# Two transformer blocks on one core: the front's order of work, the attention's turns, and constant products in TensorE's waits

## The reference

```python
# first block: layer 0 (MLA) and layer 1 (sliding window)
mem_n = rmsnorm(mem, mem_norm_g)
proj = rmsnorm(x, attn_norm_g[0]) @ mla_w_in           # 384 q rank, 256 kv rank, 32 rope, 256 cross
q  = rmsnorm(c_q, q_norm_g) @ w_uq                     # 12 heads of 64 + 32 rope
kv = rmsnorm(c_kv, kv_norm_g) @ w_ukv                  # 12 heads of 64 + 64
mix = softmax(causal(q k^T)) v                         # rope on q and on one shared key part
cross = softmax(q_cross (mem_n @ w_mem_kv)_k^T) (...)_v  # 4 heads over 256 memory rows
x = x + concat(mix, cross) @ w_o
x = x + relu(rmsnorm(x) @ w_up)**2 @ w_down            # 4096 hidden
# layer 1: the same with window attention, alibi, sinks
x = rmsnorm(x, final_norm_g)
# second block: m = silu(c) @ ada_w + ada_b gives shift, scale, gate
# layer 0: convolutions and RG-LRU, then w_out; swiglu ffn of 2816
# layer 1: qkv (1024 -> 3072), stick-breaking attention of 16 heads, w_out; swiglu ffn
```

## Time and profile before

| | us |
|---|---|
| median of 3 runs | 1308.36 |
| lowest and highest | 1306.59 and 1308.95 |
| the profiled execution | 1304.23 |
| its span | 1302.1 |
| TensorE busy | 1230.4 |
| VectorE busy | 875.4 |
| ScalarE busy | 639.2 |
| GpSimd busy | 116.9 |

### The profile page before, as it was taken

One profiled execution on the slowest core, in us unless ns is written; L12 is line 12 of the kernel. 1 busy time (PEld: TensorE's weight loads), 2 busy tenths in 40 slices (PEclk: granted clock), 3 DMA queues, 4 the chain that ended last, 5 costly groups with the idle time before them and its releaser, 6 DMA issues.

```text
span 1302.1 us, 21705 instructions
## 1 busy us (share of the span) xinstructions
PE 1230.4 (94%) x8765; PEld 1149.4 (88%) x8765; DVE 875.4 (67%) x1130; ACT 639.2 (49%) x839; POOL 116.9 (9%) x178
## 2 busy tenths in 40 slices
PE   6779999999999999999889989999979998999998
PEld 6768899988897999989789989998868778999987
DVE  5565588777885697778787677774576556554453
ACT  6526566633236566633447344433355674444332
POOL 0000001110115011111100001100000240000000
PEclk9889999999999999999989889999989999999999
DMA  8432368786862388777733548865645304456452
GB/s 308 147 108 75 127 215 290 285 291 247 277 228 91 103 284 289 256 287 267 267 121 139 165 146 272 289 218 164 220 141 193 131 1 129 136 188 193 133 177 76
DMA packets 150000, 249.83 MB, mean 192 GB/s; under 512 B 5505, under 2 KB 80618, under 8 KB 149930
## 3 DMA queue, kind: packets, MB, share of 16 engines
q1 hardware_dynamic: 135810, 198.21, 45.2%
q0 software_dynamic: 13952, 50.60, 10.7%
q10 hardware_dynamic: 168, 0.04, 0.0%
HBM read 247.79 MB, written 1.05 MB: 191 GB/s over the span
## 4 chain that ended last, share of the span: by engine, by line
PE 88%; DVE 6%; ACT 3%; issue 2%; ACTq 0%; POOL 0%; DVEq 0%; POOLq 0%
PE ps L1861 19%; PE ps L1862 19%; PE ps L1863 19%; PE ps L1881 14%; PE ps L1883 7%; DVE w_lo L1109 2%; PE ps L2128 2%; PE ps L1995 1%; PE ps L2110 1%; PE ps L2313 1%; PE ps L1926 1%; PE ps L2286 1%; PE ps L2097 1%; PE ps L1916 1%; PE ps L2323 1%
## 5 line engine op out<-in xcount | busy, mean ns | idle before, releaser
L1861 PE MATMUL ps<-h_hi,w_hi 128*128 128x256 f32 x1648 | 473.8, 287 | 19.9 <-issue 14.6
L1109 DVE TENSOR_TENSOR w_lo<-raw,w_hi 128x2048 fp32r<-128x2048 f32 (+4 forms) x196 | 412.3, 2144 | 116.3 <-ACT w_hi L703 116.1
L1862 PE MATMUL ps<-h_lo,w_hi 128*128 128x256 f32 x1648 | 470.4, 285 | 0.0
L1863 PE MATMUL ps<-h_hi,w_lo 128*128 128x256 f32 x1648 | 470.2, 285 | 0.0
L703 ACT ACTIVATE w_hi<-raw 128x2048 fp32r<-128x2048 f32 (+4 forms) x196 | 341.2, 1790 | 190.0 <-PE ps L1883 129.7
L1861 PEld LDWEIGHTS ps<-h_hi,w_hi 128*128 128x128 f32 x1648 | 318.8, 193 | 22.1 <-issue 18.7
L1862 PEld LDWEIGHTS ps<-h_lo,w_hi 128*128 128x128 f32 x1648 | 318.9, 193 | 0.1
L1863 PEld LDWEIGHTS ps<-h_hi,w_lo 128*128 128x128 f32 x1648 | 318.6, 193 | 0.1
L1881 PE MATMUL ps<-a_both,w_hi 128*128 128x512 f32 x800 | 283.7, 398 | 0.0
L1883 PE MATMUL ps<-a_both,w_lo 128*128 128x256 f32 x800 | 224.8, 281 | 0.0
L1881 PEld LDWEIGHTS ps<-a_both,w_hi 128*128 128x128 f32 x800 | 150.4, 188 | 36.5
(11 more groups left out here) (367 smaller groups left out, 1445.5 us busy)
## 6 DMA issues: line engine op xcount, KB each, us to landing
ada_raw<-in_l_ada_w POOLq DMA_DIRECT2D x96, 512.0 KB, 6.8
raw<-in_mlp_w_up SPq DMA_DIRECT2D x32, 1024.0 KB, 7.3
raw<-in_mlp_w_down SPq DMA_DIRECT2D x32, 1024.0 KB, 6.9
raw<-in_l_ffn_w_gate SPq DMA_DIRECT2D x22, 1024.0 KB, 5.5
raw<-in_l_ffn_w_up SPq DMA_DIRECT2D x22, 1024.0 KB, 8.0
raw<-in_l_ffn_w_down SPq DMA_DIRECT2D x16, 768.0 KB, 6.0
raw<-in_l_w_qkv SPq DMA_DIRECT2D x12, 1024.0 KB, 6.3
raw<-in_l_w_in SPq DMA_DIRECT2D x10, 1024.0 KB, 6.4
```

The costliest lines, as they stand in the source:

```text
L1109: nc.vector.tensor_tensor(w_lo[:, s.slot, cut], raw[:, s.slot, cut], w_hi[:, s.slot, cut].bitcast(F32), ALU.subtract).then_inc(split_lo, 1)
L1861: nc.tensor.matmul(to, sh, mh, start=first, stop=False, skip_group_check=True)
L1862: nc.tensor.matmul(to, sh, ml, start=False, stop=False, skip_group_check=True)
L1863: return nc.tensor.matmul(to, sl, mh, start=False, stop=last, skip_group_check=True)
```

## The change

SP loads `mem0` in two halves, each as soon as half of the first slot is split. `kvn` has squares of its own (`sq_kv`). On ScalarE and VectorE the front's norms are cut into steps (squares, sums, variance, root, scaling, high parts) and dealt out among the splits and copies. `w_uq` and `w_ukv` alternate between two pairs of banks. `mem0` and `mem1` go chunk by chunk. Silu is made from Exp on ScalarE and a reciprocal on VectorE; the sines move behind the last `kv_rows_out`. `mix_turn` waits for one group per pair. ScalarE makes the exponentials of heads 16 and 17 before it copies `swa_v`, and `down0`'s tenth slot (the second of `swa`) is split earlier, on VectorE in halves around `delayed_var`. `warm_up` and `keep_warm` put products of constants or of weights, whose results nobody reads, in TensorE's queue.

```diff
# SP
-            load(Slot("mem0", 0), k_major(a["w_mem_kv"][0]))
+            for half in range(2):
+                sp.wait_ge(split_lo, 2 * half + 2)
+                cut = slice(half * KD // 2, (half + 1) * KD // 2)
+                sp.dma_start(ring(raw, mem_slot.slot, KD, BANK)[:, cut, :], w_mem[:, cut, :]).then_inc(raw_loaded[mem_slot.slot], 16)
...
# ScalarE
             nc.scalar.activation(cqT[:, 0:2, :], acc(0).rearrange("p (c t) -> p c t", c=2), ACT.Copy).then_inc(acc_out[0], 1)
+            wait_source(act, "qn")
+            squares_of("qn")
             split(Slot("mem0", 0))
...
-            norm("qn", meanwhile=lambda: split(Slot("w_uq", 0)))
+            act.wait_ge(acc_out[0], turn("w_in", 1) + 1)
+            squares_of("kvn")
+            root_of("qn")
+            split(Slot("w_uq", 0), (0,))
+            high_of("qn")
+            split(Slot("w_uq", 0), (1,))
...
+            mem_keys("mem0", mem_k0)
+            root_of("kvn")
+            split(Slot("w_ukv", 0), (0,))
+            high_of("kvn")
+            q_rows_out(0)
+            split(Slot("w_ukv", 0), (1,))
+            q_rows_out(1)
+            small_columns()
+            q_rows_out(2)
+            split(Slot("mem1", 0), (0,))
+            kv_rows_out(0)
+            split(Slot("mem1", 0), (1,))
+            kv_rows_out(1)
+            kv_rows_out(2)
+            trigonometry()
...
             delayed_pair("attn1", 2)
+            split(Slot("down0", 9))
             delayed_pair("attn1", 3)
-            split(Slot("down0", 9))
...
             split(Slot("swa", 4))
+            exp_head(16)
+            exp_head(17)
             wait_part(Slot("swa", 3), 1)
...
-            heads(16, 32)
+            heads(16, 32, begun=2)
# VectorE
+            sums_of("qn")
             split(Slot("mem0", 0))
+            row_low(1, 0, m_hi, m_lo)
+            row_low(1, 1, m_hi, m_lo)
+            wait_part(Slot("w_in", 1), 1)
+            nc.vector.tensor_scalar(qx0[:, 1, :], ps[:, 1, 0:T], -HD ** -0.5, None, ALU.mult)
+            nc.vector.tensor_copy(kropeT[:, :], ps[0:ROPE, 1, T:2 * T]).then_inc(acc_out[1], 1)
+            row_low(1, 2, m_hi, m_lo)
+            row_low(1, 3, m_hi, m_lo)
+            variance_of("qn")
+            sums_of("kvn")
+            scaled("qn")
+            split(Slot("w_uq", 0))
+            mem_values("mem0", mem_v0)
+            variance_of("kvn")
+            scaled("kvn")
+            q_rows_out(0)
             split(Slot("w_ukv", 0))
             q_rows_out(1)
+            vector_constants()
+            trigonometry()
             q_rows_out(2)
+            split(Slot("mem1", 0), (0,))
+            kv_rows_out(0)
+            split(Slot("mem1", 0), (1,))
+            small_columns()
+            kv_rows_out(1)
+            kv_rows_out(2)
...
-                ada_group_done(ADA_GROUP[f"down{l}"] + 4)
+                if l:
+                    ada_group_done(ADA_GROUP["down1"] + 4)
...
+            split(Slot("down0", 9), (0,))
             delayed_var("attn1")
-            split(Slot("down0", 9))
+            split(Slot("down0", 9), (1,))
# TensorE
+UQ_BANKS, UKV_BANKS = ((4, 5), (0, 1), (4, 5)), ((0, 1), (4, 5), (0, 1))
+            def keep_warm(phase, n, bank=WARM_BANK):
+                s = Slot(phase, 0)
+                w = ring(w_hi, s.slot, s.kc, s.cols)
+                pe.wait_ge(split_lo, s.split + 2)
+                for _ in range(n):
+                    nc.tensor.matmul(ps[:, bank, 0:T], w[:, 0, 0:P], w[:, 1, 0:T], start=True, stop=True, skip_group_check=True)
+            def warm_up(n):
+                for _ in range(n):
+                    nc.tensor.matmul(ps[:, 1, 0:P], ones[:, :], ident[:, :], start=True, stop=True, skip_group_check=True)
...
+            warm_up(18)
             turn_rows(0, rows_x)
+            warm_up(6)
             as_chunks_arrive("w_in", "attn0")
...
-            memory("mem0", between="qn")
+            norm_sum_all("qn")
+            memory = [("features", (0, P)), ("rows", CROSS, CROSS, ((0, 0), (1, T)))]
+            as_chunks_arrive("mem0", "mem", work=memory, hi=m_hi, lo=m_lo, sums_after=1, sums="kvn")
...
                     for tile in range(NT):
-                        wait_acc(tile, turn(phase, g))
-                        token_rows(s, ps[:, tile, 0:n], tile, g * n, n, hi, lo).then_inc(parts_done, 1)
+                        if (phase, g) != ("w_uq", 0):
+                            wait_acc(tile, turn(phase, g) - 1)
+                        token_rows(s, ps[:, banks[g][tile], 0:n], tile, g * n, n, hi, lo).then_inc(parts_done, 1)
...
             for q in range(4):
+                if q == 2:
+                    for tile in range(NT):
+                        wait_acc(tile, turn("w_ukv", 1) + 1)
                 turn_pair(2 + q, lambda ch, t: x_again[:, t, (2 * q + ch) * P:(2 * q + ch + 1) * P]).then_inc(turned, 1)
-            memory("mem1")
+            as_chunks_arrive("mem1", "mem", work=memory, hi=m_hi, lo=m_lo)
...
+                if not begun:
+                    warm_up(4)             # in heads, after the first two scores
...
-                pe.wait_ge(o_copied, copied)
                 for q in range(4):
+                    pe.wait_ge(o_copied, copied - 3 + q)
                     turn_pair(2 + q, lambda ch, t: rows_from[:, t, (2 * q + ch) * P:(2 * q + ch + 1) * P]).then_inc(mix_turned, 1)
+            wait_acc(1, turn("mem1", 0) + 1)
+            warm_up(4)                     # ahead of the heads
...
+            keep_warm("lru_in", 6)
             norm_sum_all("final")
...
+            keep_warm("lru_in", 48)
             as_chunks_arrive("lru_in", "mix0")
...
+            keep_warm("lru_out", 20, NORM_BANK)
             as_chunks_arrive("lru_out", 2, order=LRU_PAIRS)
...
+                keep_warm(f"gate_up{l}", 11)
                 norm_sum_all(f"ffn{l}")
+                keep_warm(f"gate_up{l}", 36)
...
+            keep_warm("qkv", 5)
             norm_sum_all("mix1")
+            keep_warm("qkv", 36)
```

More of the change, by code:

```diff
@@ L142 @@
 FIRST_UP_BANKS = (2, 3)
+WARM_BANK = 3
+UQ_BANKS, UKV_BANKS = ((4, 5), (0, 1), (4, 5)), ((0, 1), (4, 5), (0, 1))
 LRU_ORDER = (4, 1, 2, 3, 0)
@@ L824, in _, with kv_rows_out @@
[L824 to L828, removed]
+            def kv_rows_out(g):
                 act.wait_ge(parts_done, Slot("w_ukv", 0).before + 2 * g + 1)
-                kv = acc(0).rearrange("p (h d) -> p h d", h=4)
+                kv = acc(UKV_BANKS[g][0]).rearrange("p (h d) -> p h d", h=4)
                 nc.scalar.activation(k_rows[:, 0, 4 * g:4 * g + 4, 0:HD], kv[:, :, 0:HD], ACT.Copy)
@@ L877, in sink_sums, with heads @@
                 nc.scalar.activation(sinkexp[:, :, :], sinkexp[:, :, :], ACT.Exp).then_inc(sink_exp, 1)
-            def heads(first, last):
+            def heads(first, last, begun=0):
                 for hc in range(first, last + 1):
-                    if hc < last:
+                    if first + begun <= hc < last:
                         exp_head(hc)
@@ L1146, in norm @@
                 wait_source(dve, name)
[L1147 to L1152 removed]
+                l, which = MODULATED[name]
+                gain_of = lambda ch: modg[:, l, which, ch:ch + 1]
                 def low(q):
@@ L1407, in _ @@
             nc.vector.tensor_copy(ckvT[:, 0, :], ps[:, 1, T:2 * T]).then_inc(acc_out[1], 1)
+            sums_of("qn")
             split(Slot("mem0", 0))
-            vector_constants()
-            for q in range(4):
-                row_low(1, q, m_hi, m_lo)
-            def during_qn():
-                wait_part(Slot("w_in", 1), 1)
-                nc.vector.tensor_scalar(qx0[:, 1, :], ps[:, 1, 0:T], -HD ** -0.5, None, ALU.mult)
-                nc.vector.tensor_copy(kropeT[:, :], ps[0:ROPE, 1, T:2 * T]).then_inc(acc_out[1], 1)
-                split(Slot("w_uq", 0))
-                trigonometry()
@@ L1421, in _ @@
-            norm("qn", between=during_qn)
-            def q_rows_out(g):
-                dve.wait_ge(parts_done, Slot("w_uq", 0).before + 2 * g + 2)
-                nc.vector.tensor_scalar(q_rows[:, 1, 4 * g:4 * g + 4, :], ps[:, 1, 0:4 * QK].rearrange("p (h d) -> p h d", h=4),
-                                        -QK ** -0.5, None, ALU.mult).then_inc(acc_out[1], 1)
-            def during_kvn():
-                mem_values("mem0", mem_v0)
-                q_rows_out(0)
-            norm("kvn", between=during_kvn)
+            row_low(1, 0, m_hi, m_lo)
@@ L1944, in four_blocks, with as_chunks_arrive @@
                     two_bank_slot(phase, j)
-            def as_chunks_arrive(phase, name, work=None, order=range(4), hi=h_hi, lo=h_lo, sums_after=None, banks=(0, 1)):
+            def keep_warm(phase, n, bank=WARM_BANK):
[7 more added lines that the diff above has]
+                    nc.tensor.matmul(ps[:, 1, 0:P], ones[:, :], ident[:, :], start=True, stop=True, skip_group_check=True)
```

(3 more changed lines are left out.)

160 lines of the change are left out of this document (89 added, 71 removed).

## The result

The changed kernel took 1271.56 us (median of 4 runs, 1270.63 to 1273.65) where the kernel before took 1308.65 (median of 4, 1306.59 to 1308.99): a ratio of 0.9722, 95% interval 0.9705 to 0.9739. Measured again on another chip it was 1272.44 against 1305.88: 0.9744 (0.9729 to 0.9759). The first measurement gives 37.1 us, the second 33.4. The prediction was 1278 (1269 to 1290), faster. Of the 32 timed executions of the kernel before, two took 1331.5 and 1333.3 us at a mean granted clock of 0.956 and 0.954, and no comparison here uses them.

The account below looks back on a forecast made before the run. TensorE, busy 94% of 1302.1 us, was taken as the bound, with only its waits and lower-clock time to win. Front 18.7, attention 5.5 and fillers 6.3 make 30.5; 1308.4 - 30.5 = 1278, range 1269 to 1290.

Parts of the forecast that it names:

- the offset of 4.1: Whole kernel: the runs' median is 4.1 us above the profiled execution, carried over to the forecast of 1278.
- rival B: Front: new waits overlap or vanish; front 23 to 25, fillers 8, 38 us in all, so 1270; chance 0.14.
- the 6.8: Front, at 53.4: TensorE's wait of 6.8 us behind ScalarE's `mem_k`, forecast to go entirely.
- The new waits: Front: waits the change itself brings to TensorE, behind splits, banks and copies; 6.7 us with the last copy.
- the last copy: Front's end, before the first scores: TensorE waits 0.7 us for it, counted among the new losses.
- 71.9: Front: TensorE's work between the first product (14.89) and 112.2, products and transposes together, 71.9 us of 97.3.
- the 25.4 reckoned: Front: time TensorE loses in the kernel before, in waits and at half rate, 25.4 us of a 97.3 stretch.
- Rival A: Front: in-order queues bite more than walked; front 12, total 20 to 24 us, so 1286; chance 0.16.
- Rival D: Front: norm, split and copy chain only displaced, `w_ukv` and `mem1` wait as long; 1289; chance 0.07.
- between the front and the end no DMA is on the chain: After the front: no transfer binds, so a shift won at the front is kept to the end.
- rival E: Norms, `lru_out`, start: fillers run at half rate and outlast their waits, costing 20 us; kernel slower; chance 0.04.
- Rival C: Norms: fillers don't hold the clock and win nothing; the rest, 24 to 25 us, stands; 1284; chance 0.07.

Follow-up runs that it names:

- the second trace: The unedited changed kernel profiled and timed once more, on another chip: 1272.44 us, against 1305.88 for the kernel before.
- `swa_kT` first: Against the changed kernel, VectorE scales `swa_kT` before the products with `ada_raw` and not behind them: 1271.58 us.

## Why the prediction came out as it did

**The sum.** It said 30.5 us; the profiled executions are 30.6 apart, the medians 33.4 and 37.1. Two things lie between 30.6 and 37.1. The profiled execution of before was 4.4 below its median (4.1 by the median that the prediction had), and that of the changed kernel 2.1 above its own. The failed step is the one that took the offset of 4.1 us over to the kernel after. What the runs show in its place is that the offset goes with the clock, and the change brings the clock to 0.995 to 0.998: the executions of before that took 1305.8 us and more ran at a mean granted clock of 0.975 to 0.978, those near the profile at 0.979 or 0.980. An estimate: 0.0035 of 1305 us is 9.1 us more at half rate, which costs up to 4.6. That this half rate lay behind the waits is argued and not shown, for no trace of an execution at 0.975 was kept. The 2.1 is the changed kernel's own spread; 1.1 of it is what `qkv`'s fillers lost in that execution and not in the repeated one. The median lies nearer to rival B's 1270, but not by B's way: the front gave 20.3 and not 23, the fillers 5.2 and not 8.

That 30.5 met 30.6 is in part luck. By the traces the span became 30.1 shorter: the front gave 20.3 for 18.7, the attention 5.4 for 5.5, the fillers 5.2 for 6.3, and 0.85 was lost in `w_o0`, which the sum didn't have.

**Front: 19.1 to the first scores, measured 20.4.** First product 13.88 (predicted 13.8), `w_uq` straight behind `mem0` at 51.59 (51.6), the 6.8 gone. The new waits were 6.7 and came to 2.9: `cqT` 0.4 (0.7), `v_rows` 0.9 (2.0), `mla_qT` 1.6 (1.7), none for `w_ukv`'s split (1.0), its banks (0.6) and the last copy (0.7). The clock did not fall before `mem1` (0.7). Those 4.5 did not all come out as gain, because the term for TensorE's work was too small. From the first product to the first scores the changed kernel takes 78.0 us; without the 2.9 of waits and 1.1 of fillers that is 74.0 of work, where the sum had 71.9. The part that the trace shows best: `w_uq`'s products are 0.173 us apart and not 0.16, `w_ukv`'s 0.23 and not 0.215, 1.2 together. So less was idle before than the 25.4 reckoned, and the wait for `w_ukv`'s split is hidden: the split ended when I said, 61.2, and TensorE got there at 61.39. The fillers ahead of the scores take the last 1.1. Rival A (queues bite more) had the right places and the wrong size; moving two entries of the queues took the remaining 2.5 out and showed that the order was the cause. Rival D is refuted by the 51.59.

**Attention: 5.5, measured 5.4.** The turns gave 1.1, 1.1 and 2.0 (predicted 1.0, 1.0, 1.3), the exponentials 1.0 (1.2). The split gave 1.4 (1.0), and 1.1 of it was lost at once at the first scores. Here a second step failed: that "between the front and the end no DMA is on the chain". VectorE stands before the transfer of `ada_raw` with the scaling of `swa_kT` behind it in its queue. It did so in the kernel before too, for 1.81 us, but there the first scores waited only 0.14. The transfer came 20.8 us earlier in the changed kernel, where TensorE came 21.9 earlier, and so took what the split had won; `swa_kT` first won 0.9 of it back. The table of waits named no transfer because it was VectorE that stood before it. The 0.85 lost in `w_o0` is another matter: its products were 0.113 us apart in the trace of before and 0.118 in that of after, 192 times. Both values occur in the traces of the same kernel; what decides is open.

**Fillers: 6.3, measured 5.2 in the first trace.** `gate_up` 1.6 and 1.6 (1.4 each), `lru_out` 2.0 (2.2), `lru_in` 0.5 lost (0), `qkv` 0.5 (1.3). At `lru_in` fillers at half rate outlasted the wait by 1.0, and a wait of 0.76 for `h_lo` followed, as foreseen. `qkv` is rival E in small: 1.7 won behind its fillers and 1.2 lost in them. In the second trace `qkv` gained 1.1 more. Rival C is refuted: taking all constants out costs 8.8 to 9.7 us, where their forecast, with 2.4 at the start, was 8.7.

## What to carry to other kernels

Where waits of a few microseconds make a kernel's clock fall, its executions scatter: take the medians and the mean granted clock of several before a sum made against one profile is carried over to the median. An edit that wins a microsecond is lost at the next engine that stands before a transfer with other work queued behind it, so put what TensorE needs ahead of what waits for a DMA. A sum that meets the measured time can still be made of misses: compare it place by place. And when many small steps move at once, look in the new trace for wide splits ahead of small copies: two moves of a line each gave 3.5 us here.

## What the runs showed of the hardware

Transposes of a constant in FP32 raised the granted clock to 1.00 at the start of the kernel and held it there through what were waits of 4.4 us, as products did. Without fillers the clock behind one and the same wait stayed at 0.50 (1.2 GHz) for 16 to 27 products (`gate_up0`), or in other executions did not fall (`lru_out`, `w_in`). The same FP32R products of 256 columns were 0.113 us apart in some executions and 0.118 in others for the whole of `w_o0` or `w_o1`, at a granted clock of 1.00 in both. That is 0.86 us for each of the two, in kernels whose edits don't touch them, so two single traces can differ by as much.
